# Four edits to a two-block transformer kernel: a mixer by seven quarter products, shorter vector chains, gathers over three expert groups, and the order of additions

## The reference, cut to what matters

```python
def first_block(x, ...):                     # DEPTH = 2
    for i in range(DEPTH):
        y = rms_norm(h, norm1[i])
        y = mixer_a(y, ...) if i == 0 else mixer_b(y, b_win, b_conv, b_wout)
        h = h + y
        h = h + mlp_sq_relu(rms_norm(h, norm2[i]), mlp_w1[i], mlp_w2[i])   # D_FF = 4096
def second_block(x, c, positions, ...):      # DEPTH = 2
    for l in range(DEPTH):
        sh1, sc1, gt1, sh2, sc2, gt2 = split(silu(c) @ w_mod[l] + b_mod[l])
        h = rms_norm_2(x, norm1_g[l]) * (1.0 + sc1) + sh1
        # retention, differential attention and gated linear attention of h @ w_in[l]
        x = x + gt1 * (mixed @ w_out[l])
        h2 = rms_norm_2(x, norm2_g[l]) * (1.0 + sc2) + sh2
        idx, gates = route(h2, router_w, router_b)   # 8 groups of 4 experts: best group, its best 2
        x = x + gt2 * moe(h2, idx, gates, w_gate, w_up, w_down)            # 32 experts, D_EXPERT = 512
```

## Time and profile before

| | us |
|---|---|
| median of 2 runs | 2132.64 |
| lowest and highest | 2132.39, 2132.88 |
| span of the profiled execution, first to last instruction | 2131.9 |
| TensorE busy in it (94% of the span) | 2014.4 |
| VectorE busy in it (47%) | 993.5 |
| ScalarE busy in it (16%) | 332.7 |
| mean HBM to SBUF rate over the span | 293 GB/s |

### The profile page before, as it was taken

How to read it: one execution, slowest core, us unless ns; L and a number is a source line. 1 busy time by engine, 2 the same in 40 slices (tenths; PEclk the granted TensorE clock), 3 DMA queues, 4 the chain that set the end, 5 groups by cost and what they waited for, 6 DMA issues and landing times.

```text
span 2131.9 us, 26296 instructions
## 1 busy us (share of the span) xinstructions
PE 2014.4 (94%) x10846; PEld 1352.5 (63%) x10846; DVE 993.5 (47%) x1960; ACT 332.7 (16%) x729; POOL 0.2 (0%) x4
## 2 busy tenths in 40 slices
PE   8999999999999999999999998888999999988888
PEld 5999988999888999757734333333657644333333
DVE  4888863888333788355432222222256522222212
ACT  1343431000000000123201000000314101000000
POOL 0000000000000000000000000000000000000000
PEclk9999999999999999999999999999999999999999
DMA  7333446688345589342789999999934699999997
GB/s 317 130 135 132 141 156 248 247 320 320 138 158 214 214 320 337 120 178 85 294 355 400 429 426 428 429 428 426 384 141 177 238 402 405 427 426 428 427 428 328
DMA packets 117873, 625.53 MB, mean 293 GB/s; under 512 B 5760, under 2 KB 8448, under 8 KB 85632
## 3 DMA queue, kind: packets, MB, share of 16 engines
q1 hardware_dynamic: 116752, 619.06, 72.8%
q10 hardware_dynamic: 1008, 4.87, 0.6%
HBM read 622.86 MB, written 1.05 MB: 293 GB/s over the span
## 4 chain that ended last, share of the span: by engine, by line
PE 74%; DMA 18%; DVE 5%; ACT 1%; issue 1%; SPq 0%; DVEq 0%
PE ps L2880 13%; PE ps L2271 10%; PE ps L2297 8%; PE ps L2354 7%; PE ps L2234 6%; PE ps L2918 6%; DMA ring<-in_w_up 5%; PE ps L2548 4%; DMA spare<-in_w_down 4%; DMA spare<-in_w_gate 4%; DMA spare<-in_w_up 4%; PE ps L2541 3%; PE ps L2720 2%; PE ps L2339 2%; DMA ring<-in_w_down 2%; PE ps L2427 1%
## 5 line engine op out<-in xcount | busy, mean ns | idle before, releaser
L2880 PE MATMUL ps<-ring,work_rows 128*64 128x512 f32 x1248 | 445.9, 604 | 28.8 <-DMA ring<-in_w_up 12.7
L2880 PE MATMUL ps<-arena,work_rows 128*64 128x512 f32 x584 | 262.9, 603 | 22.8 <-DMA ring<-in_w_up 10.9
L2880 PEld LDWEIGHTS ps<-ring,work_rows 128*64 128x64 f32 x1248 | 139.5, 139 | 225.4 <-issue 222.2
L2918 PE MATMUL ps<-ring,arena 128*64 128x512 f32 x608 | 214.0, 602 | 12.3 <-DMA ring<-in_w_down 5.4
L2271 PE MATMUL ps<-arena,ring 128*128 128x256 f32 x1024 | 224.7, 379 | 0.0
L2271 PEld LDWEIGHTS ps<-arena,ring 128*128 128x128 f32 x1024 | 192.6, 189 | 27.4
L2354 PE MATMUL ps<-ring,work_rows 128*128 128x192 f32 x840 | 147.7, 327 | 0.4 <-ACT arena L929 0.4
L2880 PEld LDWEIGHTS ps<-arena,work_rows 128*64 128x64 f32 x584 | 78.5, 138 | 95.8 <-issue 91.1
L2050 DVE TENSOR_SCALAR arena<-arena 128x512 f32<-128x512 f32 x32 | 13.7, 428 | 265.9 <-ACT arena L1227 265.9
L2354 PEld LDWEIGHTS ps<-ring,work_rows 128*128 128x128 f32 x840 | 136.0, 190 | 1.5 <-issue 0.6
L2918 PE MATMUL ps<-arena 128*64 128x512 f32 x288 | 127.2, 594 | 8.9 <-DMA ring<-in_w_down 6.7
(11 more groups left out here) (409 smaller groups left out, 2538.0 us busy)
## 6 DMA issues: line engine op xcount, KB each, us to landing
ring<-in_mlp_w SPq DMA_DIRECT2D x32, 2048.0 KB, 13.1
ring<-in_w_up SPq DMA_DIRECT2D x32, 2048.0 KB, 34.7
ring<-in_w_gate SPq DMA_DIRECT2D x28, 2048.0 KB, 34.9
arena<-in_w_mod SPq DMA_DIRECT2D x24, 2048.0 KB, 8.0
ring<-in_w_down SPq DMA_DIRECT2D x24, 2048.0 KB, 36.8
arena<-in_w_gate SPq DMA_DIRECT2D x20, 2048.0 KB, 26.8
ring<-in_a_wqkv SPq DMA_DIRECT2D x24, 1536.0 KB, 7.4
arena<-in_w_down SPq DMA_DIRECT2D x18, 2048.0 KB, 28.0
```

The costliest lines, as they stand in the source:

```text
L2880: e = te.matmul(bank(b)[SB * h:SB * h + SB], xs(k, col, SB), slabs.chunk(m + h, k), start=(k == 0), stop=(k == KD - 1), skip_group_check=True)
L2918: e = te.matmul(bank(6 + o)[SB * h:SB * h + SB], ueT[a][:, P * k + SB * h:P * k + SB * h + SB], slabs.tile(m + h).rearrange("p (k n) -> p ...
```

## The change

- **Mixer B by seven.** Slabs 1 to 5 of mixer B are multiplied with seven quarter products each (`b_unit`, 112 instructions of 128 columns in place of 64 of 256), with sums on VectorE (`b_weight_sums`, `b_token_sums`), copies on ScalarE (`b_partials`) and joins (`b_joined`). Two sets of PSUM banks alternate. The output projection starts with the first half of its rows (`b_out`) before the convolution of the second half is done.
- **Shorter chains.** `rsqrt` is one Newton turn of three steps and one cubic turn of four, in place of nine steps. The score of a group is the highest of its six pair sums. `first_best` compares and weighs in one instruction for each half of the tokens. ScalarE copies the logits. The ranks are signalled before the counts, which go to another bank, and the slots of the first two groups are made straight from them. Fewer fills stand there (`FILL` 4 to 2, then 2 to 1). Between the blocks the last of the three folds is left to TensorE, and `permute` moves from before the sums to behind the spread.
- **Spread gathers.** The pieces 1, 2 and 3 are gathered in expert groups 1, 2 and 3, one in each; `layer_scales` and `run_masks` move from after group 1 to after group 3.
- **Order and rounding.** In the MLPs each quarter product adds its four chunks from last to first, and the inverse frequencies of the rotary tables are rounded once, on the host.

```diff
-FILL = 4
+FILL = 2
...
+            def b_partials(q, out):
+
+                a, c, b = b_banks[q % 2]
+                for n, (e, src) in enumerate(((0, a), (2, c), (1, a), (3, a))):
+                    act.wait_ge(s_product, 4 * BY_SEVEN + 28 + 4 * q - 4 + n + 1)
+                    sc.activation(b_seven[q % 2][e], src, ACT.Copy).then_inc(s_copied, 1)
+                ring.wait_done(act, B_WIN + q)
+                if q == 3:
+                    act.wait_ge(u_ready, 1)
+                elif q == 4:
+                    act.wait_ge(y_ready, 1)
+                sc.activation(out[:, 2:4, 0:P], a, ACT.Copy).then_inc(s_joined, 1)
...
+                act.wait_ge(t_logits, lay + 1)
+                sc.activation(logits[0:E], bank(6)[0:E, 0:S], ACT.Copy).then_inc(t_copied, 1)
...
-                newton(tok_root, tok_t, tok_mean, 1)
-                dve.wait_ge(t_logits, lay + 1)
-                ve.tensor_copy(logits[0:E], bank(6)[0:E, 0:S]).then_inc(t_copied, 1)
-                newton(tok_root, tok_t, tok_mean, 2)
+                newton(tok_root, tok_t, tok_mean)
+                cubic(tok_root, tok_t, tok_mean)
...
+        def cubic(y, t, x):
+
+            own.step(ve.tensor_tensor(t, y, y, ALU.mult))
+            own.step(ve.scalar_tensor_tensor(out=t, in0=t, scalar=CUBIC, in1=x, op0=ALU.mult, op1=ALU.mult))
+            own.step(ve.scalar_tensor_tensor(out=t, in0=t, scalar=-1.25 / CUBIC, in1=t, op0=ALU.add, op1=ALU.mult))
+            own.step(ve.scalar_tensor_tensor(out=y, in0=t, scalar=1.875, in1=y, op0=ALU.add, op1=ALU.mult))
...
+            def b_token_sums():
+
+                b = [[h3[:, 4 * k:4 * k + 4, P * t:P * t + P] for t in range(2)] for k in range(2)]
+                dve.wait_ge(x_summed, 3)
+                own.inc(ve.tensor_tensor(h_sum[0], b[0][1], b[0][0], ALU.subtract))
+                own.step(ve.tensor_tensor(h_sum[2], b[1][1], b[0][1], ALU.subtract))
+                own.step(ve.tensor_tensor(h_sum[1], b[1][1], h_sum[0], ALU.subtract))
+                own.step(ve.tensor_tensor(h_sum[3], b[1][0], h_sum[1], ALU.subtract))
+
+            def b_weight_sums(q):
+
+                ring.wait_landed(dve, B_WIN + q)
+                if q >= 3:
+                    ring.wait_done(dve, B_WIN + q - 2)
+                w, t = wcols(B_WIN + q), b_sum[q % 2]
+                a11, a12, a21 = w[:, 0:4, 0:S], w[:, 4:8, 0:S], w[:, 0:4, S:2 * S]
+                own.step(ve.tensor_tensor(t[0], a21, w[:, 4:8, S:2 * S], ALU.add))
+                own.inc(ve.tensor_tensor(t[1], t[0], a11, ALU.subtract))
+                own.step(ve.tensor_tensor(a21, a11, a21, ALU.subtract))
+                own.step(ve.tensor_tensor(t[2], a12, t[1], ALU.subtract))
+                if q > 1:
+                    dve.sem_inc(s_summed, 1)
+
+            def b_joined(q, out):
+
+                a, c, b = b_banks[q % 2]
+                part = b_seven[q % 2]
+                ring.wait_done(dve, B_WIN + q)
+                dve.wait_ge(s_copied, 4 * BY_SEVEN + 28 + 4 * q)
+                own.inc(ve.tensor_tensor(out[:, 0:2, 0:P], b, part[0], ALU.add))
+                own.inc(ve.tensor_tensor(out[:, 0:2, P:S], c, part[1], ALU.add))
+                own.step(ve.tensor_tensor(out[:, 2:4, P:S], part[2], part[3], ALU.add))
+                dve.wait_ge(s_joined, BY_SEVEN + q)
+            b_weight_sums(1)
+            token_mean(2, 7)
+            b_token_sums()
+            dve.sem_inc(s_summed, 1)
             own.step(ve.reciprocal(tok_inv, tok_mean))
             rsqrt(tok_root, tok_t, tok_mean)
             diagonals(0, tok_inv, False)
             diagonals(NT, tok_root, True)
             square_scale, scale = [scale_b[:, n, :].unsqueeze(1).broadcast_to([P, 4, S]) for n in range(2)]
             conv = par1("conv")
+            b_weight_sums(2)
             for s in range(2):
-                ring.wait_done(dve, B_WIN + 3 * s + 1)
+                if s:
+                    b_joined(3, tmp_a.rearrange("p (k t) -> p k t", k=4))
+                    dve.sem_inc(c_copied, 1)
+                    b_weight_sums(5)
...
-                own.inc(ve.tensor_tensor(hi, quads[:, :, 0:2], quads[:, :, 2:4], ALU.max))
-                own.step(ve.tensor_tensor(lo, quads[:, :, 0:2], quads[:, :, 2:4], ALU.min))
-                own.inc(ve.tensor_tensor(top, hi[:, :, 0], hi[:, :, 1], ALU.max))
-                own.inc(ve.tensor_tensor(second_, hi[:, :, 0], hi[:, :, 1], ALU.min))
-                own.step(ve.tensor_tensor(gsum, lo[:, :, 0], lo[:, :, 1], ALU.max))
-                own.step(ve.tensor_tensor(second_, second_, gsum, ALU.max))
-                own.step(ve.tensor_tensor(gsum, top, second_, ALU.add))
-
-                def first_best(values, out, iota, n, signal=None):
-
-                    own.step(ve.tensor_reduce(best, values, AX, ALU.max))
-                    own.step(ve.tensor_tensor(out, values, best.unsqueeze(2).broadcast_to([P, NT, n]), ALU.is_equal))
-                    own.step(ve.scalar_tensor_tensor(out=out, in0=out, scalar=-100.0, in1=iota, op0=ALU.mult, op1=ALU.add))
+                own.inc(ve.tensor_tensor(pairs[:, :, 0:3], quads[:, :, 0:3], quads[:, :, 1:4], ALU.add))
+                own.inc(ve.tensor_tensor(pairs[:, :, 3:5], quads[:, :, 0:2], quads[:, :, 2:4], ALU.add))
+                own.step(ve.tensor_tensor(pairs[:, :, 5:6], quads[:, :, 0:1], quads[:, :, 3:4], ALU.add))
+                own.inc(ve.tensor_reduce(gsum, pairs, AX, ALU.max))
+
+                def first_best(values, out, iota, n, signal=None, among=None):
+
+                    own.step(ve.tensor_reduce(best, values if among is None else among, AX, ALU.max))
+                    for r in range(NT):
+                        e = ve.scalar_tensor_tensor(out=out[:, r, :], in0=values[:, r, :], scalar=best[:, r:r + 1], in1=iota,
+                                                    op0=ALU.is_equal, op1=ALU.mult)
+                        own.inc(e)
+                    own.settle()
...
+                dve.wait_ge(t_ranks, lay * 2 + 1)
+                for r in range(NT):
+                    own.inc(ve.tensor_tensor_reduce(own_rank[:, r, :], bank(5)[:, NG * r:NG * r + NG], group_of[:, r, :],
+                                                    1.0, 0.0, ALU.mult, ALU.add, rank_of[:, r:r + 1]))
+                own.settle()
+                for r in range(NT):
+                    e = ve.scalar_tensor_tensor(out=sel[:, r, 0:2, :],
+                                                in0=con2("slotj")[:, 0:SB].unsqueeze(1).broadcast_to([P, 2, SB]),
+                                                scalar=rank_of[:, r:r + 1],
+                                                in1=group_of[:, r, 0:2].unsqueeze(2).broadcast_to([P, 2, SB]),
+                                                op0=ALU.is_equal, op1=ALU.mult)
+                e.then_inc(first_ready, 1)
...
-                    if g == 1 and lay + 1 < DEPTH:
+                    group(home, g * GROUP_SLABS, g, g * SB, slot_gate[:, 2 * g:2 * g + 2], c=g if g < PIECES else 0)
+                    if g == MIDDLE - 1 and lay + 1 < DEPTH:
...
+            pe.wait_ge(x_folded, folded(n, folds(n)))
             for h in range(2):
                 for r in range(NT):
                     e = te.matmul(bank(b)[:, r:r + 1], tmp[:, S * h + P * r:S * h + P * r + P], com("ones")[:, 0:1],
-                                  start=(h == 0 and r == 0), stop=(h == 1), skip_group_check=True)
+                                  start=(h == 0 and r == 0), stop=(h == 1 and folds(n) == 3), skip_group_check=True)
+            if folds(n) < 3:
+                fill(2, 7)
+                pe.wait_ge(x_squared, 4 * n + 4)
+                for h in range(2):
+                    for r in range(NT):
+                        e = te.matmul(bank(b)[:, r:r + 1], tmp[:, 1536 + S * h + P * r:1536 + S * h + P * r + P],
+                                      com("ones")[:, 0:1], start=False, stop=(h == 1), skip_group_check=True)
...
-                        for k in range(4):
+                        for k in (3, 2, 1, 0):
...
+            def b_unit(q):
+
+                slab, at = B_WIN + q, 4 * BY_SEVEN + 28 + 4 * q - 4
+                w, t, (pa, pc, pb) = wcols(slab), b_sum[q % 2], b_banks[q % 2]
+                a = [[w[:, 4 * k:4 * k + 4, S * f:S * f + S] for k in range(2)] for f in range(2)]
+                b = [[h3[:, 4 * k:4 * k + 4, P * t:P * t + P] for t in range(2)] for k in range(2)]
+
+                def product(out, left, right, start=False):
+
+                    for o in range(2):
+                        for k in range(4):
+                            e = te.matmul(out[:, o, :], left[:, k, P * o:P * o + P], right[:, k, :],
+                                          start=(start and o == 0 and k == 0), stop=False, skip_group_check=True)
+                    return e
+                ring.wait_landed(pe, slab)
+                if q == 2 or q == 5:
+                    pe.wait_ge(c_copied, q // 3 + 1)
+                elif q == 3:
```

(58 more changed lines are left out.)

170 lines of the change are left out of this document (92 added, 78 removed).

## The result

The changed kernel takes 2109.49 us (2109.39 and 2109.59), the kernel before 2132.64. The ratio is 0.9882, with a 95% interval from 0.9859 to 0.9905. The profiled span is 2107.6 us against 2131.9, with the mean granted clock at 0.988 against 0.990.

A forecast was written before the change was run, and what follows sets the result against it. TensorE's chain was taken to bound everything before the expert stages, and DMA at 428 GB/s those stages. Terms 8.0 + 2.5 + 0.4 + 2.5 + 3.8 + 5.2 = 22.4 off 2132.6 gave 2110.2 us; 2104 to 2121 holds 8 in 10.

The forecast's parts named there:

- Mixer B, 8.0: Mixer B: five units by seven save 6.6 us, output projection in the convolution's gap 1.4; bounds 8.5 and 3.
- 30.0 against 37.5 us: Mixer B: VectorE's work for three units is 30.0 us against 37.5 on TensorE, so the cover holds.
- VectorE late: Rival, 0.08: in mixer B four of five units wait for sums; gain 15.8 us, time 2116.8.
- the slower rival: Rival, 0.02: uncovered weight loads bind mixer B's units; 2161 us; the whole loses from 0.149 us an instruction.
- Shorter chains, 2.5: Mixer A: shorter rsqrt cuts each of six TensorE waits for join_v by 0.42 us; 2.5 us, bounds 0 and 3.
- Between the blocks, 2.5: MLP's end to projection: earlier sums and kept-up clock gain 2.7 us, permute costs 0.2; bounds 3.5 and -0.7.
- Routing, 1.9 a layer: Routing: 0.8 from Newton turns and copy, 0.6 to the mask, 0.5 to the gather; both layers 3.8 us.
- The clock falls: Rival, 0.07: fewer fills leave TensorE idle in routing, 4 us a layer, 2.5 not won between blocks; time 2120.7.
- Gathers, 5.2: Expert group 1: spread gathers remove DMA lulls of 3.2 and 2.8 us; 5.2 of 6.0 taken, bounds 6 and -2.
- DMA keeps its time: Rival, 0.15: gathers free slabs sooner but DMA's lull moves; gain 17.2 us, time 2115.4.
- Order and rounding, nothing: MLP chunk order and rotary rounding: the same instructions on the same operands, costing nothing.
- 0.7 around it: Whole kernel before: median of the runs 2132.6 us read as 0.7 around the profiled span of 2131.9.

The follow-up runs named there:

- e2: Changed kernel with mixer B back in full units and the output projection behind the whole convolution; 2118.12 us.
- e6: Changed kernel with two more 128x1024 subtractions in each of mixer B's five weight sums; 2107.5 us.
- e7: Changed kernel with four more 128x1024 subtractions in each of mixer B's five weight sums; 2118.8 us.
- e5: Changed kernel with one more Newton turn behind the inverse roots of q and k in mixer A alone; 2112.79 us.
- e3: Changed kernel with the old order between the blocks (three folds, permute ahead of the sums, two fills behind the spread), shorter root kept; 2114.13 us.
- e11: Changed kernel without any dummy matmul in the routing stage; 2110.87 us.
- e1: Changed kernel with the three gathers back in expert group 1, and layer_scales and run_masks back behind that group; 2114.79 us.
- e4b: Changed kernel with chunks of quarter products added first to last and inverse frequencies rounded twice, as before; 2108.88 us.
- e8: Changed kernel without the two fills between the two parts of the sums between the blocks; 2109.43 us.
- e9: Changed kernel with a fill behind the sums in both MLPs and fills around group 0's second transposes in both layers; 2107.13 us.

## Why the prediction was right

The forecast was 2110.2 and the time 2109.49. Going by its steps:

- **Mixer B, 8.0.** It came to 8.03. The 0.112 us for an instruction of 128 columns held in the mixer (12.51/112), and the cover held: TensorE waits for nothing. Undone alone it gives back the same (e2), and the cover stands two more sums a unit (2.4 us) and not four (e6, e7), where my sum of 30.0 against 37.5 us for three units gave 2.5 a unit. *VectorE late* is refuted, and so is the slower rival, which needed 0.149 us an instruction. The 81 ns against 56 of the Trainium skill (page "TensorE: Matmul & The Clock Gate", section "Back-to-back issue gap"), taken as a ratio, would have made 17.4 us a unit; this kernel's float32 instructions didn't follow it, at 0.112 us against 0.216 for twice the columns.
- **Shorter chains, 2.5.** 2.39 from the second chunk on (2.46 with the earlier start), from 0.87 to 0.48 a wait; e5 shows the opposite sign at the same rate. The 0.4 in the second layer's first norm came to 0.39.
- **Between the blocks, 2.5.** 2.21. From the MLP's end to the spread it took 8.64 and takes 5.67: 2.97 gained, where I had 2.7; the clock stayed up and VectorE's chain took the 2.4 us that I gave it. From the spread to the projection it is 3.20 against 2.44 (e3, whose stage is that of before): 0.76 lost to `permute` and its fill, where I had 0.2. That term was mis-sized.
- **Routing, 1.9 a layer.** 1.91 in both, read from the two chains; no run undoes the shorter routing by itself. *The clock falls* did not happen with the fills that are left, and does with none (e11).
- **Gathers, 5.2.** 6.7; the term was mis-sized. I had worked out 6.0 from the lulls and taken less, as a part could move. Nothing moved: the windows are full, and e1 brings back 3.0 and 3.1 (without its fall of the clock). *DMA keeps its time* is refuted. With the gathers in group 1 the stage took 373.59 in layer 1 before, and 373.61 and, less its fall of the clock, 373.6 in e1; only layer 0 before took 374.23. So about 0.6 of the 6.7 belongs to that one execution, and the gathers are worth about 3.1 a layer, near to the 6.0 of the lulls.
- **Not priced**, 0.7 in the second block's mixer and group 0.
- **Order and rounding, nothing.** As forecast (e4b).

The errors, +0.03, 0, -0.3, 0, +1.5 and +0.7 in us of gain, sum to 1.9 and make the 24.3 between the spans. By the medians the gain is only 0.75 over the forecast, as the span before was that of a slow execution. My *0.7 around it* was a wrong reading, but the sum started from the median and so did not need it. That the total was met within 0.7 is therefore in part luck, and so is the chip: on the second one the time was 2108.16, but the gain 28.6 where I had 22.4, and the sum has no term for that. Each mechanism stands by its own stage. Executions of the unaltered kernel differed by up to 2.6 us on one chip (2106.11 to 2108.67), those of e3 by 6.0, of e11 by 7.2 and of the kernel before by 9.1, so smaller errors are seen only in the stages.

## What to carry to other kernels

Where the chain of waits goes through one engine without gaps, a removed step counts in full and can be read to a tenth of a microsecond from like code elsewhere in the trace; where it goes through DMA, count only the lull in the rate, and count it whole if slabs come free sooner by more than the lull. Compare by the length of stages from mark to mark, not by whole times, when executions differ by more than a term of the sum. When a wait of TensorE is priced, add what the clock may cost behind it. Check that a profiled execution is a typical one before its span is used.

## What the runs showed of the hardware

- A fall of TensorE's clock behind an idle gap of about 1.2 us came in 12 of 48 cases, at 1.6 to 1.7 us each. Behind longer gaps it came often, but not always: behind 2.01 us between the blocks in both executions that have the gap (before and e3), behind 1.82 us in both layers of e11, behind 1.39 us in e8 and behind the long wait of e7, but behind the 2.08 us before the second pair's slabs in group 1 only in one of four cases (layer 1 of e1, and not its layer 0 nor either layer before). The Trainium skill, page "TensorE: Matmul & The Clock Gate", section "Why this matters for your kernels", advises against idle gaps between bursts of matmuls; what the runs add is that even a short gap can be followed by the lower level, and that one of 2 us need not be.
- The start of the kernel scatters: the second chunk of mixer A begins between 48.67 and 53.30 us in fourteen profiled executions, with the first slab's load taking 8.09 to 10.13 us.
- A few dummy matmuls at the right place were worth 1.13 us (e8) to 2.9 us (e11). At a wrong one they delayed what followed by 0.72 (e9), which the layer had made up by its end, where DMA sets the pace.
